# FFN blocks of a two-block transformer step on one core: both up slots' wide products first, then both slots' narrow products

## The reference, cut to what matters

```python
def conv_ffn(h, w_up, conv_w, conv_b, w_down):
    u = causal_depthwise_conv(h @ w_up, conv_w, conv_b)   # 3 taps
    g, val = jnp.split(u, 2, axis=-1)
    return (jax.nn.silu(g) * val) @ w_down
```

## Time and profile before

| what | value |
|---|---|
| median of three executions | 1485.76 us |
| the profiled execution's own time | 1485.7 us |
| its span in the trace | 1483.9 us |
| TensorE (PE) busy | 1470.4 us, 99% |
| GpSimd (POOL) busy | 1015.1 us, 68% |
| VectorE (DVE) busy | 884.8 us, 60% |
| ScalarE (ACT) busy | 779.5 us, 53% |

### The profile page before, as it was taken

The page is one execution under the profiler, slowest core; times in us unless marked ns, Lnnn a source line. Parts: engine busy times, 40 slices in busy tenths (PEclk is TensorE's granted clock), DMA queues, the critical chain, the costliest instruction groups (busy, mean ns, idle before and its releaser), DMA issues.

```text
span 1483.9 us, 26057 instructions
## 1 busy us (share of the span) xinstructions
PE 1470.4 (99%) x8780; PEld 1297.5 (87%) x8780; DVE 884.8 (60%) x2165; ACT 779.5 (53%) x1321; POOL 1015.1 (68%) x807
## 2 busy tenths in 40 slices
PE   9999999999999999999999999999999999999997
PEld 7789999999999888888888888888899889888886
DVE  4663389989998655543333333335677534377776
ACT  6576554454444545444444444448666656645454
POOL 6759888975555000049999999998944466598996
PEclk9999999999999999999999999999999999999999
DMA  7536567653333555566666666656642444466664
GB/s 257 159 98 190 176 187 234 194 165 114 115 114 127 186 199 191 192 190 188 188 187 188 188 186 188 188 183 183 201 127 86 152 133 143 135 186 189 189 192 128
DMA packets 137573, 252.86 MB, mean 170 GB/s; under 512 B 16464, under 2 KB 18896, under 8 KB 136848
## 3 DMA queue, kind: packets, MB, share of 16 engines
q1 hardware_dynamic: 135392, 243.79, 53.3%
q10 hardware_dynamic: 1872, 6.41, 1.2%
q0 software_dynamic: 224, 1.54, 0.3%
HBM read 248.54 MB, written 3.15 MB: 170 GB/s over the span
## 4 chain that ended last, share of the span: by engine, by line
PE 74%; POOL 13%; issue 10%; DVE 1%; ACT 1%; DMA 0%; POOLq 0%; SPq 0%; ACTq 0%; DVEq 0%
POOL w_lo L500 12%; PE bank L533 11%; PE bank L535 11%; PE bank L534 11%; PE bank L629 8%; PE bank L1484 4%; PE bank L630 4%; PE bank L975 4%; PE bank L542 3%; PE bank L547 3%; PE bank L543 3%; PE bank L1487 2%; PE bank L551 2%; PE bank L556 2%; PE bank L552 2%
## 5 line engine op out<-in xcount | busy, mean ns | idle before, releaser
L500 POOL TENSOR_TENSOR w_lo<-ring,w_hi 128x512 fp32r<-128x512 f32 x784 | 997.6, 1298 | 453.3 <-ACT w_hi L1541 444.3
L1541 ACT CAST w_hi<-ring 128x1024 fp32r<-128x1024 f32 x452 | 474.2, 1050 | 499.7 <-PE bank L535 224.0
L533 PE MATMUL bank<-w_hi,act_hi 128*128 128x512 f32 x596 | 234.8, 394 | 0.8 <-DVE act_lo L2700 0.4
L535 PE MATMUL bank<-w_hi,act_lo 128*128 128x512 f32 x596 | 233.0, 391 | 0.0
L534 PE MATMUL bank<-w_lo,act_hi 128*128 128x512 f32 x596 | 232.5, 390 | 0.0
L629 PE MATMUL bank<-h_both,w_hi 128*128 128x512 f32 x512 | 182.7, 397 | 0.0
L2721 DVE TENSOR_REDUCE work<-bank 128x256 f32<-128x512 f32 x64 | 44.3, 692 | 169.4 <-PE bank L630 169.4
L630 PE MATMUL bank<-h_both,w_lo 128*128 128x256 f32 x512 | 143.6, 280 | 0.0
L542 PE MATMUL bank<-h_both,w_hi 128*128 128x256 f32 x568 | 141.6, 287 | 0.0
L543 PE MATMUL bank<-h_both,w_hi 128*128 128x256 f32 x568 | 139.2, 283 | 0.0
L533 PEld LDWEIGHTS bank<-w_hi,act_hi 128*128 128x128 f32 x596 | 111.9, 188 | 25.6 <-POOL w_lo L500 1.1
(11 more groups left out here) (470 smaller groups left out, 2747.5 us busy)
## 6 DMA issues: line engine op xcount, KB each, us to landing
ring<-weights_in SPq DMA_DIRECT2D x910, 256.0 KB, 2.9
mem_kv<-arena ACTq DMA_DIRECT2D x2, 1024.0 KB, 7.2
arena<-mem_kv ACTq DMA_DIRECT2D x2, 1024.0 KB, 7.0
ring<-weights_in SPq DMA_DIRECT2D x8, 200.0 KB, 2.4
ring<-weights_in SPq DMA_DIRECT2D x8, 144.0 KB, 2.2
xres<-x_in SPq DMA_DIRECT2D x2, 512.0 KB, 5.4
arena<-mem_in POOLq DMA_DIRECT2D x1, 1024.0 KB, 7.1
arena<-rows_in ACTq DMA_DIRECT2D x2, 512.0 KB, 4.1
```

The lines of the kernel that those rows point to most:

```text
L500: nc.gpsimd.tensor_tensor(w_lo[:, k, at], ring[:, k, at], w_hi[:, k, at].bitcast(F32), ALU.subtract).then_inc(s[done], 1)
L533: pe.matmul(out_, a[0], b[0], start=start, stop=False, **kw)
L535: return pe.matmul(out_, a[1], b[0], start=False, stop=stop, **kw)
L1541: nc.scalar.copy(w_hi[:, k, :], ring[:, k, :]).then_inc(s["hi_made"], 1)
```

## The change

The loop over the two halves is cut in two. First both slots' wide products, each half behind its wait for `hi_made`; then both slots' narrow products, each half behind its wait for `split`, with `spent` raised after each half's narrow products as before.

```diff
@@ -1482,6 +1482,8 @@
                     pe.wait_ge(s["hi_made"], n + (half + 1))
                     for c in range(KD):
                         pe.matmul(to, w_hi[:, (k + half) % NS, c * P:(c + 1) * P], h_both[:, c, :], start=(c == 0), stop=False, skip_group_check=True)
+                for half in range(2):
+                    to = bank[:, 4 + 2 * u + half, :]
                     pe.wait_ge(s["split"], n + (half + 1))
                     for c in range(KD):
                         mm = pe.matmul(to[:, 0:T], w_lo[:, (k + half) % NS, c * P:(c + 1) * P], h_both[:, c, 0:T],
```

## The result

Six executions of the changed kernel took 1495.12 to 1497.89 us, median **1495.85 us**; six of the kernel before 1484.71 to 1487.66, median 1485.67. The ratio is 1.0069 (95% interval 1.0058 to 1.0079): the change costs 0.7%, 10.2 us. The forecast was 1495.5 us.

What follows compares the result with a forecast made beforehand. TensorE, busy 99%, was taken as the bound, with GpSimd's splits nearly as long. Entry 0.13, sixteen periods at 0.509 and end 1.5 summed to 9.8 us on 1485.7: 1495.5 us, range 1491.0 to 1499.0.

Steps and rivals of the forecast that it cites:

- The late release: Gate slot released 1.81 us later, delaying copy, silu, cast and splits: down products can begin 14.78 us after first wide product.
- The loop over two periods: Chain plus slow down products closes over two periods: 17.63 us, 8.815 each against 8.306, +0.51 us a period.
- The rival of one absorbed stall (A): TensorE stalls once, then the pace returns to 8.27 us a period: 1487.7 us; chance 0.11 with its milder ends.
- the step from silu to split: From the silu to the split of V: 1.53 us in one parity, 1.44 in the other, taken as 1.49.
- The regular stalls of 0.4 to 0.5 us: Waits for the split before the first down product in nearly each period, 7 to 8 us in all.
- The end: Last down products wait for the last block's act_lo, 12.52 us after the last first wide product: +1.5 us.
- The entry: First periods of the FFN: third down products start at 1326.57 instead of 1326.44, +0.13 us.
- ScalarE's wait of 2.88 us: Wait before a cast at the entry, taken as beside the V cast; if in order behind it, up to 1.4 us more.
- Rival (B): A longer chain: the entry's wait in order and 8.94 us a period, 1499 us; chance 0.07 beyond the bounds.
- TensorE's own order: One switch between wide and narrow products goes in each period: at most 0.03 us saved, 0.6 over twenty.
- The clock (D): Short gaps in each period take TensorE's granted clock to 1.2 GHz for a stretch: +44 us, 1540 us; chance 0.04.

Runs made afterwards that it cites:

- e1: The changed kernel with ScalarE's cast of the next value slot moved ahead of the silu; 1486.64 us, ratio 1.0009.
- e2: The changed kernel with all down products but the last block's in two parts, four w_lo products behind the split wait; 1485.34 us, ratio 1.0001.
- e3: The kernel before, TensorE's order untouched, with ScalarE's gate copy waiting for the value slot's release, 2.80 us later; 1506.12 us, ratio 1.0142.
- e7: The kernel before with all down products but the last block's in two parts, the w_lo ones behind the split wait; 1484.57 us, ratio 0.9996.
- e4: Half of the change: the gate's narrow products after four of the value's eight wide ones, gate released 0.91 us later; 1487.23 us, ratio 1.0015.

## Why the prediction was right, point by point

**The late release: right, and shown.** The chain was given as 14.78 us and measured 14.82. e1 cuts it at the silu, e2 moves its deadline, e3 makes it longer with the old order; each did what the chain says.

**The loop over two periods: right, and shown** by e3's pair of 18.64 us and the slope of 10 us per microsecond. The rival of one absorbed stall (A) is out. In the changed kernel the period was (1469.90 - 1328.50) / 16 = 8.838 us, where 8.815 was forecast: 141.40 against 132.90 us before, +8.5 instead of +8.1. The mis-sized term is the step from silu to split. I took the mean of the two parities, 1.49 us, but each parity closes its own loop, and the slower one rules. Seven pairs of the faster parity took 1460.63 - 1337.48 = 123.15 us, 17.59 each, eight of the slower 141.40, 17.68 each. So the stalls drift apart, from 0.33 and 0.16 us around 1380 to 0.65 in one parity and none listed in the other around 1449. The regular stalls of 0.4 to 0.5 us that were forecast did not come: the weight loads' waits in the sixteen periods ran from 0.19 to 0.91 us and two periods had none, though their sum, 7.5 us, lies in the 7 to 8 that were forecast.

**The end: right.** It took 12.65 us from the last s to the last down group, 12.52 forecast, 11.03 before. The wait is the one that the forecast named, on the last act_lo:

```profile
1469.90 3.79 PE L1484 MATMUL bank<-h_both,w_hi 128*128 128x512 f32 x16
...
1482.55 0.47 PE L533 MATMUL bank<-w_hi,act_hi 128*128 128x512 f32 x1 [0.86 <-DVE act_lo L3123]
```

**The entry: +0.08 us** (1302.12 to 1328.50, 26.38 us, against 26.30 before), +0.13 forecast. ScalarE's wait of 2.88 us in the earlier trace rows did not come back: in the changed kernel the two casts there follow each other. Rival (B), with 1.4 us more here and 8.94 us a period, is out. Why that wait went is not shown.

**TensorE's own order: right in sign.** 0.03 us a period were expected at most, e2 gives 0.02, against the kernel before and against e7. So the order of the groups is worth something, if little, other than by the formula that the prediction takes from the section "Back-to-back issue gap" of the page "TensorE: Matmul & The Clock Gate" of the Trainium skill. That section gives the formula for a single gap, not for a stream of weight loads and products as here, a limit that the prediction leaves out; its own sum goes by the measured steps. A length of 2.07 us for sixteen narrow products agrees with the earlier trace rows.

**The clock (D): out.** TensorE's products waited thirteen times for a split in the changed kernel, up to 0.7 us, and nineteen times in e3, up to 1.3 us. From 1303 to 1462 us the granted clock was 1.00 in both, the level of 2.4 GHz. The loss from frequent small gaps that the page "TensorE: Matmul & The Clock Gate", section "A second HAM failure mode", of the Trainium skill describes, for a bf16 kernel that cycles through PSUM banks, is not seen in any of these runs.

**What the forecast did not see** is the second path of the release, cast of G and three splits, at 13.78 us against a deadline of 13.80. In the changed kernel it lay behind the longer path: GpSimd there is through with G and then idles for 1.00 us until V is cast. In e1 the periods alternate between 8.28 or 8.29 and 8.34 to 8.38 us; in the mean they are 0.04 us longer than in e2, and I put this down to the second path, which is argued and not tested. That GpSimd had a share of 91% was read the earlier trace rows, but the path was not added up.

## What to carry to other kernels

When work of one engine is regrouped, its own time may hardly change, and what counts is when it releases its inputs: follow the release through the other engines' lists in their order, up to the point where the engine itself waits, and compare with the room there. Where the chain closes over k periods, each microsecond past the room should cost a k-th in every period; it was measured here for k = 2 only. The cure need not undo the regrouping: a cast moved ahead of a wait, or a wait put behind the products that do not need it, was enough.

## What the runs showed of the hardware that was not expected

After a wait at the down slot TensorE's first products come slowly: 0.33 us to the second instead of 0.23 (1317.76 to 1318.09 in the kernel before) and 2.85 us for the group instead of 2.74. The forecast had this size from the earlier trace rows; new is that e4 pays it also where the trace lists no idle time. Twenty such restarts would be some 2 us, an estimate from 20 x 0.11.

Code that alternates between two buffers (here `u`) need not have two equal periods. In the kernel before ScalarE's cast of V starts 0.40 us after the silu in one parity (1385.50 to 1385.90) and 0.32 in the other, from 1377.20 to this row:

```profile
1377.52 1.04 ACT L1541 CAST w_hi<-ring 128x1024 fp32r<-128x1024 f32 x1
```

The changed kernel shows it too, 0.40 (1389.71 to 1390.11) and 0.33 us (1380.83 to 1381.16). The parity with the later cast is the one whose loop set the pace. Why the two differ is open.
